# The first tap of 44 blocks moves from VectorE to ScalarE, and VectorE sums the second rows of all pairs 1 to 47

## The chip, the cores and the metric

One NeuronCore of a Trainium2 chip runs the whole program. The metric is the device time of one launch in microseconds: before the change the median of three runs is 2565.99 us (2560.9 to 2567.07). TensorE multiplies matrices into PSUM, VectorE (DVE) and ScalarE (ACT) work elementwise, GpSimd (POOL) issues the gathers of rows, SyncE (SP) issues the loads of weights. The engines run side by side and meet at semaphores.

## What the reference computes

Two transformer blocks over 512 positions of width 1024. The part that matters here is the gated feed-forward of the first block,

```
up = causal_dwconv(h2 @ ffn_w_up, ffn_conv_w, ffn_conv_b)   # 3 taps, 5632 columns
a, b = split(up);  x = x + gate2 * ((silu(a) * b) @ ffn_w_down)
```

and the expert layer at the end of the second, in which every position and each of 8 heads picks 16 of 16384 experts:

```
u = expert_u[experts];  act = gelu(sum_d u * h);  v = expert_v[experts]
out = sum_k gate_k * act_k * v_k
```

## The kernel before

The sequence is worked on in two halves of 256 positions. The first half runs ahead: its expert layer begins while the second half still has its first block's feed-forward to do. That work of the second half is put between the steps of the expert layer, by tables written out by hand.

The unit of the expert layer is a **pair** p: two gathered rows per position (each a 128x2048 f32 tile, `expert_u` and `expert_v` side by side, 1.05 MB), 16 choices of a head make 8 pairs, 256 pairs in all. GpSimd gathers rows 2p and 2p+1 into a ring of 9 slots (`ring_e`); it may refill a slot when its old row has been used. VectorE forms the row products of both rows (`row_dot`, L2267). ScalarE turns them into weights and into diagonal matrices (`weigh_pair`, L1467 to L1478). TensorE adds diagonal times row into two PSUM banks (`row_pair`): two products of 128x512 for each row, each of them two records of the trace. For a pair that stands in the table `SIDE` TensorE does the first row only, ScalarE makes one diagonal only, and VectorE adds weight times second row to an SBUF tile, two pairs later (`side_row`, 128x1024); TensorE takes that tile in once for every 64 pairs. Before the change `SIDE` holds 1 to 23, then every other pair from 25 to 39, then 40 to 47, and some later ones.

After its part of pair p every engine does what the tables put **beside** it. `UP_AT` places the 44 up blocks of the second half: three blocks in two pairs, in pairs 1 to 16 and 22 to 35 (odd pairs two, even pairs one, with small exceptions). `DOWN_AT` places 24 down blocks in pairs 17 to 21 and 35 to 45. For an up block m at pair `UP_AT[m]`:

- TensorE multiplies it (`expand`, 128x258, 16 records), into one of three PSUM banks in turn. It waits for the weights, which SyncE loads when the block three before is done (`half_done`, three slots `w2`), and for the bank, until the block three before has been read out (`evicted`: for an up block `fy_ready`).
- VectorE at `UP_AT[m]` + 2 applies the three taps of the convolution from PSUM (`expanded`): one `tensor_scalar` with the bias, then two `scalar_tensor_tensor`; the last counts `fy_ready`.
- ScalarE at + 3 takes the tanh for the gate (`tanh_gate`), VectorE at about + 4 multiplies gate and value (`gate_value`).

Each engine works in this order strictly. So VectorE, which waits in `expanded` for the end of a block of TensorE two pairs back, can be two pairs ahead of TensorE and no more. From pair 48 on there are further such blocks, and later stages only have the expert layer.

Of the kernel before, what the change touches and what calls it, by code (L numbers as in the profile page):

```python
# [15 lines left out]
ACT = mybir.ActivationFunctionType  # L16
# [15 lines left out]
FT = FF // P  # L32
# [13 lines left out]
HF = S // 2  # L46
# [37 lines left out]
def ffn_at(i):  # L84

    return 1 + 2 * i // 3


UP_AT = [ffn_at(b if b < 24 else b + KT) for b in range(2 * FT)]
# [10 lines left out]
            {m: 102 + 2 * m if m < 4 else 112 + 4 * (m - 4) for m in range(16)}]  # L100


SIDE = [*range(1, 24), *range(25, 40, 2), *range(40, 48), *range(56, 62), *range(83, 88, 2), *range(88, 96)]


def sides(p):

    return sum(q < p for q in SIDE)


def by_tensor(g):

    return g - sum(2 * q + 1 < g for q in SIDE)

# [25 lines left out]
TURN = {b: t for t, b in enumerate(ORDER)}  # L140
# [32 lines left out]
def build(nc, a, out):  # L173
    ctx = ExitStack()
    with ctx:
# [33 lines left out]
        def par(name, i=0, n=1):  # L209
            b = PARAM[name][0] + i  # L210
            return param[:, b:b + n]
# [78 lines left out]
        yg = wring[:, 3072:3584].rearrange("p (u n) -> p u n", n=HF)  # L290
        yv = wring[:, 3584:4096].rearrange("p (u n) -> p u n", n=HF)
# [44 lines left out]
        PS = ctx.enter_context(nc.psum_tensor("PS", [P, 8, S], F32))  # L336
# [7 lines left out]
        half_done = sem("half_done")  # L344
# [23 lines left out]
        ff_ready = sem("ff_ready")  # L368
# [67 lines left out]
        qkv_ready = sem("qkv_ready")  # L436
# [26 lines left out]
        vec_step = sem("vec_step")  # L463
# [32 lines left out]
        def bank(name, half, m):  # L496
            return 2 + TURN[name, half, m] % SLOTS2
# [54 lines left out]
        def _(pe):  # L552
# [446 lines left out]
            def row_pair(p, start, stop):  # L999
# [3 lines left out]
                if start:  # L1003
                    pe.wait_ge(hr_ready, 4)
                    if p:
                        pe.wait_ge(prow_ready, 2 * (p // TILE))
                rows = range(1 if p in SIDE else BATCH)
                for k in rows:
# [128 lines left out]
        def _(act):  # L1137
            n = Count()
            A = nc.scalar.activation
# [217 lines left out]
            def square_block(s, k):  # L1357
# [6 lines left out]
                    act.wait_ge(sq3_used, SUMS3[s] + k - 3)  # L1364
                A(sq4[:, k % 4, :], xT[:, k, HF:] if s else xT[:, k, :HF], ACT.Square).then_inc(sq3_ready, 1)

            def tanh_gate(t):

                act.wait_ge(fy_ready, 2 * FT + 2 * t + 1)
                if t >= 2:  # L1370
                    act.wait_ge(ff_ready, FT + t - 1)
                A(st[t % 2], yg[:, t % 2, :], ACT.Tanh, scale=0.5).then_inc(sa_ready, 1)
# [6 lines left out]
            def apply3(s):  # L1379

                shift, col = (0, 2) if s == 1 else (24, 3)
                if s == 0:
                    act.wait_ge(mod_ready, 4)
                for k in range(KT):
                    act.wait_ge(normed3, KT * s + k + 1)
                    h = hv[:, 1, k, :] if s else hv[:, 0, k, :]
                    A(h, h, ACT.Identity, bias=mod[:, 1, shift + k:shift + k + 1], scale=eff[:, col, k:k + 1]).then_inc(h3_ready, 1)
# [73 lines left out]
            def weigh_pair(p, r):  # L1461

                b = p % NB
                act.wait_ge(dots_ready, BATCH * (p + 1))
                if p - NB in SIDE:
                    act.wait_ge(side_used, sides(p - NB + 1))
# [5 lines left out]
                act.wait_ge(w_ready2, BATCH * p + 1)  # L1472
                if p in SIDE:
                    A(diag[:, b, 0, :], ident, ACT.Copy, scale=wts[:, b, 0:1]).then_inc(diag_ready, 1)
# [32 lines left out]
            def beside(p):  # L1507

                c, q = divmod(p, TILE)
                if c and q == 0:  # L1510
                    keep_tile(c - 1)
                if p == 3:
                    keep_scores(0, EARLY - 1)
                for s in range(2):
                    for m, at in QUERY_AT[s].items():
                        if p == at + 2:
                            keep_query(s, m)
                        if p == at + 5:
                            keep_scores(s, m)
                for m, at in enumerate(WIN_AT):  # L1520
                    if p == at + 2:
                        keep_block(1, m)
                for g, at in enumerate(POOL_AT):
                    if p == at + 2:
                        keep_pool(1, g)
                if p == LN_AT + 2:
                    keep_mean(1)
                if p == LN_AT + 3:
                    ln_squares(1)
                if p == LN_AT + 6:  # L1530
                    ln_root(1)
                if p == LN_AT + 7:
                    ln_tanh(1)
                for m, at in enumerate(WOUT_AT):
                    if p == at + 2:
                        square_block(2, m)
                if p == NORM_AT + 2:
                    root3(2)
                if p == NORM_AT + 3:
                    apply3(2)  # L1540
                for t in range(FT):
                    if p == UP_AT[2 * t] + 3:
                        tanh_gate(t)
                for m, at in enumerate(DOWN_AT):
                    if m // KT == CHUNKS - 1 and p == at + 2:
                        square_block(1, m % KT)
                if p == MID_AT + 2:
                    root3(1)
                if p == MID_AT + 3:
                    apply3(1)  # L1550
                if p - 2 in BROW_AT:
                    keep_brow(BROW_AT.index(p - 2))
                if p - 2 in XROW_AT:
                    keep_x(*XROW_AT[p - 2])
                if p - 2 in FIN_AT:
                    deviation(FIN_AT[p - 2])
                if 0 < c < NC - 1 and q == 50:
                    keep_rows(c + 1, 0, 7)
                if 0 < c < NC - 1 and q == 53:
                    keep_rows(c + 1, 1, 7)  # L1560
# [21 lines left out]
        def _(dve):  # L1582
            n = Count()
# [5 lines left out]
            def ts(o, x, s1, s2, op0, op1):  # L1589
                return V.tensor_scalar(o, x, s1, s2, op0, op1)  # L1590
# [21 lines left out]
            MUL, ADD, SUB, MAX, MIN = ALU.mult, ALU.add, ALU.subtract, ALU.max, ALU.min  # L1612
# [358 lines left out]
            for i in range(FT // 2):  # L1971
                ada_steps(4 * i, 4 * i + 4)
                for u in range(2):
                    for z in range(2):
# [3 lines left out]
                        o = (y0 if z == 0 else y1)[:, u, :]  # L1978
# [141 lines left out]
            def expanded(m):  # L2120

                t, z = divmod(m, 2)
                o, b = (yg, yv)[z][:, t % 2, :], bank("up", 1, m)
                dve.wait_ge(half_done, TURN["up", 1, m] + 1)
                ts(o, PS[:, b, 2:HF + 2], par("fconv", 3 * m + 2), par("fbias", m), MUL, ADD).then_inc(vec_step, 1)
                dve.wait_ge(vec_step, n(vec_step))
                stt(o, PS[:, b, 1:HF + 1], par("fconv", 3 * m + 1), o, MUL, ADD).then_inc(vec_step, 1)
                dve.wait_ge(vec_step, n(vec_step))
                stt(o, PS[:, b, 0:HF], par("fconv", 3 * m), o, MUL, ADD).then_inc(fy_ready, 1)
                dve.wait_ge(fy_ready, n(fy_ready))  # L2130
# [196 lines left out]
            def beside(p):  # L2327

                c, q = divmod(p, TILE)
                if p - 2 in SIDE:  # L2330
                    side_row(p - 2)
                for g in range(4):
                    if p == WIN_AT[g] + 3:
                        pool_diff(1, g)
                for t in range(4):
                    if p == WIN_AT[5 + 2 * t] + 3:
                        gated(1, t)
                for i, at in enumerate(DW_AT):
                    if p == at:
                        tap(1, i)  # L2340
                if p == LN_AT + 3:
                    ln_center(1)
                if p == LN_AT + 7:
                    ln_scale(1)
                if p == LN_AT + 8:
                    ln_silu(1)
                for m, at in enumerate(BRANCH_AT):
                    if p == at + 2:
                        merge(1, m)
                for m, at in enumerate(WOUT_AT):  # L2350
                    if p == at + 2:
                        add_block(1, m)
                if p == NORM_AT + 3:
                    norm3(2)
                if p == MID_AT + 3:
                    norm3(1)
                for t in range(FT):
                    if p == max(UP_AT[2 * t] + 4, UP_AT[2 * t + 1] + 3):
                        gate_value(t)
                for m, at in enumerate(UP_AT):  # L2360
                    if p == at + 2:
                        expanded(m)
                for m, at in enumerate(DOWN_AT):
                    if p == at + 2:
                        add_part(m)
                if p in FIN_AT:
                    finish(FIN_AT[p])
                if p - 3 in FIN_AT:
                    scale_rows(FIN_AT[p - 3])
# [183 lines left out]
```

## Time and profile before

| | |
|---|---|
| median of three runs | 2565.99 us |
| profiled execution | 2566.99 us, span 2565.3 us |
| TensorE busy | 2293.6 us (89%) |
| VectorE busy | 1719.5 us (67%) |
| ScalarE busy | 695.7 us (27%) |
| GpSimd busy | 618.9 us (24%) |
| moved by DMA | 748.97 MB, mean 292 GB/s |
| chain that ended last | PE 62%, DMA 23%, DVE 9%, ACT 4% |

The span is the time from the first to the last instruction. "Busy" is the time in which an engine executes. The chain is followed back from the last instruction, at each step to what released it, so its shares say what the time was spent on. In the 40 equal slices of the page (64 us each) the expert layer begins in the seventeenth, at 1023 us; pair 24 begins on TensorE at 1243 us, pair 40 at 1368 us, pair 48 at 1412 us.

### The profile page before, as it was taken

The numbers are of one execution on the slowest core, as the hardware profiler recorded it, in microseconds if no ns is written. First come the engines' busy times: TensorE is split into PE (matmuls) and PEld (weight loads), VectorE is DVE, ScalarE is ACT, GpSimd is POOL, SyncE is SP. The second block draws the span as 40 slices with busy tenths as digits, with TensorE's granted clock in tenths as the row PEclk, the third lists the DMA queues.
The fourth block names the chain that finished last, engine by engine and source line by source line (L and its number), as shares of the span: only waits on it lengthen the run. The fifth ranks groups of instructions, "written<-read, shape, count | busy, mean of one in ns | idle before, by whom it ended". The sixth has DMA issues, their size and how long they took to land.

```text
span 2565.3 us, 25633 instructions
## 1 busy us (share of the span) xinstructions
PE 2293.6 (89%) x8418; PEld 1491.4 (58%) x8418; DVE 1719.5 (67%) x3782; ACT 695.7 (27%) x1990; POOL 618.9 (24%) x612
## 2 busy tenths in 40 slices
PE   3999998899999998899999998999998877777776
PEld 2544685748888887677777565675444433232222
DVE  6753564617655853778887799877667666676664
ACT  2221122413101111221222322424333333333332
POOL 2100000000001000222332333434444434344342
PEclk7999997899999999999999999999999999999999
DMA  8621102025666433999999999999999999999997
GB/s 304 228 80 57 33 1 66 1 98 197 237 219 240 148 128 124 388 343 369 409 374 390 392 380 371 376 410 409 419 419 419 420 420 420 418 418 420 419 418 295
DMA packets 130584, 748.97 MB, mean 292 GB/s; under 512 B 14497, under 2 KB 14497, under 8 KB 64673
## 3 DMA queue, kind: packets, MB, share of 16 engines
q0 software_dynamic: 87552, 587.24, 57.4%
q1 hardware_dynamic: 42912, 160.26, 17.6%
q8 instruction: 60, 0.98, 0.2%
q14 instruction: 60, 0.48, 0.1%
HBM read 745.35 MB, written 2.10 MB: 291 GB/s over the span
## 4 chain that ended last, share of the span: by engine, by line
PE 62%; DMA 23%; DVE 9%; ACT 4%; issue 2%; another core or an unknown queue 0%; POOL 0%; DVEq 0%; ACTq 0%; POOLq 0%
PE PS L554 61%; DMA arena<-experts_dram,ecur 21%; DVE arena L2267 3%; DVE h_all L1593 2%; DMA arena<-ada_dram 1%; DVE arena L1593 1%; ACT arena L1471 1%; DVE arena L1587 1%; ACT L1467 1%; DVE h_all L1587 1%; ACT const L1478 0%; ACT const L1476 0%; DMA ring<-up_dram 0%; DMA ring<-down_dram 0%; ACT arena L1467 0%
## 5 line engine op out<-in xcount | busy, mean ns | idle before, releaser
L554 PE MATMUL PS<-arena,const 128*128 128x512 f32 (+2 forms) x1872 | 879.5, 614 | 179.6 <-ACT const L1478 165.6
L554 PE MATMUL PS<-h_all,ring 128*128 128x256 f32 (+2 forms) x3584 | 884.2, 405 | 10.5 <-ACT h_all L1166 4.0
L2426 POOL DMA_INDIRECT arena<-experts_dram,ecur x512 | 567.8, 1109 | 1162.7 <-PE PS L554 758.8
L2267 DVE CUSTOM_DVE_ANT_0 arena<-arena 128x1024 f32<-128x1024 f32 x512 | 626.0, 1223 | 293.5 <-DMA arena<-experts_dram,ecur 289.3
L554 PEld LDWEIGHTS PS<-h_all,ring 128*128 128x128 f32 x3584 | 681.8, 191 | 221.7 <-issue 135.6
L554 PEld LDWEIGHTS PS<-arena,const 128*128 128x128 f32 (+1 forms) x1872 | 353.6, 195 | 626.2 <-issue 361.4
L1467 ACT ACTIVATE arena<-arena 128x2 f32<-128x2 f32 x255 | 51.8, 203 | 846.9 <-DVE arena L2267 846.5
L554 PE MATMUL PS<-arena,ring 128*128 128x256 f32 (+1 forms) x960 | 245.3, 417 | 3.7 <-DVE arena L1587 2.6
L554 PEld LDWEIGHTS PS<-arena,ring 128*128 128x128 f32 x960 | 186.8, 195 | 63.9 <-issue 36.6
L554 PE MATMUL PS<-arena 128*128 128x128 f32 (+2 forms) x1088 | 157.1, 305 | 8.6 <-DVE arena L1587 3.5
L554 PEld LDWEIGHTS PS<-arena 128*128 128x128 f32 (+1 forms) x1088 | 143.4, 208 | 28.2 <-issue 8.4
L1593 DVE SCALAR_TENSOR_TENSOR arena<-arena,silc 128x512 f32<-128x512 f32 x168 | 126.3, 752 | 18.0 <-DMA arena<-ada_dram 12.3
L1471 ACT ACTIVATE arena<-arena 128x1 f32<-128x1 f32 x510 | 122.3, 287 | 8.4
L1593 DVE SCALAR_TENSOR_TENSOR xT<-PS,mod,xT 128x256 f32<-128x256 f32 (+1 forms) x56 | 29.0, 520 | 128.3 <-PE PS L554 128.2
L2408 POOL DMA_DIRECT2D arena<-ada_dram x4 | 2.1, 528 | 384.6 <-ACT arena L1294 384.6
L1587 DVE TENSOR_TENSOR arena<-arena 128x256 f32<-128x256 f32 (+9 forms) x185 | 86.4, 467 | 5.4 <-ACT arena L1212 2.7
L2413 POOL DMA_DIRECT2D arena<-ada_dram x44 | 23.2, 528 | 266.3 <-DVE arena L1593 266.3
L1478 ACT ACTIVATE const<-const,arena 128x128 f32<-128x128 f32 x199 | 76.8, 386 | 0.0
L1476 ACT ACTIVATE const<-const,arena 128x128 f32<-128x128 f32 x199 | 76.8, 386 | 0.0
L1593 DVE SCALAR_TENSOR_TENSOR arena<-arena 128x1024 f32<-128x1024 f32 (+3 forms) x93 | 75.8, 815 | 0.6 <-ACT arena L1471 0.3
L1590 DVE TENSOR_SCALAR arena<-PS,param 128x256 f32<-128x256 f32 (+1 forms) x56 | 32.9, 588 | 58.8 <-PE PS L554 57.8
L1593 DVE SCALAR_TENSOR_TENSOR arena<-PS,param,arena 128x255 f32<-128x255 f32 (+3 forms) x124 | 69.4, 559 | 4.4
(246 smaller groups left out, 1591.0 us busy)
## 6 DMA issues: line engine op xcount, KB each, us to landing
arena<-ada_dram POOLq DMA_DIRECT2D x96, 512.0 KB, 5.2
ring<-up_dram SPq DMA_DIRECT2D x88, 512.0 KB, 3.5
ring<-w_in_dram SPq DMA_DIRECT2D x80, 512.0 KB, 3.6
ring<-query_dram SPq DMA_DIRECT2D x32, 512.0 KB
ring<-w_out_dram SPq DMA_DIRECT2D x24, 512.0 KB, 4.0
ring<-down_dram SPq DMA_DIRECT2D x16, 704.0 KB, 4.9
ring<-branch_dram SPq DMA_DIRECT2D x16, 512.0 KB
arena<-experts_dram,ecur POOLq DMA_INDIRECT x512
```

The lines of the kernel that those rows point to most:

```text
L554: return nc.tensor.matmul(o, l, r, start=start, stop=stop)
L1467: A(wts[:, b, :], dots[:, b, :], ACT.Gelu_apprx_tanh).then_inc(gelu_ready, 1)
L1471: A(wts[:, b, k:k + 1], wts[:, b, k:k + 1], ACT.Copy, scale=gcur[:, r % 3, j:j + 1]).then_inc(w_ready2, 1)
L1476: A(diag[:, b, 0, :], ident, ACT.Copy, scale=wts[:, b, 0:1]).then_inc(act_step, 1)
L1478: A(diag[:, b, 1, :], ident, ACT.Copy, scale=wts[:, b, 1:2]).then_inc(diag_ready, 1)
L1587: return V.tensor_tensor(out=o, in0=x, in1=y, op=op)
L1590: return V.tensor_scalar(o, x, s1, s2, op0, op1)
L1593: return V.scalar_tensor_tensor(out=o, in0=x, scalar=s_, in1=y, op0=op0, op1=op1)
L2267: V.tensor_tensor_reduce(out=u, in0=u, in1=hrow[:, (r // HEADS) % 2, :], scale=1.0, scalar=0.0, op0=MUL, op1=ADD, accum_out=dots[:, p % NB ...
L2408: pool.dma_start(ring_2[:, j, :], a["ada_2"][j]).then_inc(slot_2_ready[j], 16)
L2413: pool.dma_start(ring_2[:, j, :], a["ada_2"][bass.ds(i * SLOTS + j, 1)].rearrange("o p n -> p (o n)")).then_inc(slot_2_ready[j], 16)
L2426: nc.gpsimd.indirect_dma_start(out=ring_e[:, g % RING, :], out_offset=None, in_=a["experts"], in_offset=bass.IndirectOffsetOnAxis(ap=ecur[ ...
```

## The change

The table `SIDE` now holds all pairs 1 to 47, so the eight even pairs 24 to 38 are added: TensorE leaves their second rows out, VectorE sums them. The first tap with the bias is done by ScalarE with an `Identity` activation from PSUM (`up_tap`), at `UP_AT[m]` + 2. VectorE does the other two taps at + 3, after a wait for ScalarE's tap instead of TensorE's block. `gate_value` stands at + 4 after the later of the two blocks.

```diff
-SIDE = [*range(1, 24), *range(25, 40, 2), *range(40, 48), *range(56, 62), *range(83, 88, 2), *range(88, 96)]
+SIDE = [*range(1, 48), *range(56, 62), *range(83, 88, 2), *range(88, 96)]
@@ ScalarE
+            def up_tap(m):
+
+                t, z = divmod(m, 2)
+                act.wait_ge(half_done, TURN["up", 1, m] + 1)
+                if t >= 2:
+                    act.wait_ge(ff_ready, FT + t - 1)
+                A((yg, yv)[z][:, t % 2, :], PS[:, bank("up", 1, m), 2:HF + 2], ACT.Identity, bias=par("fbias", m),
+                  scale=par("fconv", 3 * m + 2)).then_inc(qkv_ready, 1)
...
+                for m, at in enumerate(UP_AT):
+                    if p == at + 2:
+                        up_tap(m)
@@ VectorE
-                dve.wait_ge(half_done, TURN["up", 1, m] + 1)
-                ts(o, PS[:, b, 2:HF + 2], par("fconv", 3 * m + 2), par("fbias", m), MUL, ADD).then_inc(vec_step, 1)
-                dve.wait_ge(vec_step, n(vec_step))
+                dve.wait_ge(qkv_ready, 12 + m + 1)
                 stt(o, PS[:, b, 1:HF + 1], par("fconv", 3 * m + 1), o, MUL, ADD).then_inc(vec_step, 1)
...
-                    if p == max(UP_AT[2 * t] + 4, UP_AT[2 * t + 1] + 3):
+                    if p == max(UP_AT[2 * t], UP_AT[2 * t + 1]) + 4:
                         gate_value(t)
                 for m, at in enumerate(UP_AT):
-                    if p == at + 2:
+                    if p == at + 3:
                         expanded(m)
```

TensorE's queue at pairs 23 to 26, before (`PS<-arena,const` are the rows times diagonals, x2 for one row and x4 for two; `PS<-h_all,ring` are up blocks, 8 products each):

```order
L554 MATMUL PS<-h_all,ring 128x258 x16
L554 MATMUL PS<-arena,const 128x512 x4
L554 MATMUL PS<-h_all,ring 128x258 x8
L554 MATMUL PS<-arena,const 128x512 x2
L554 MATMUL PS<-h_all,ring 128x258 x16
L554 MATMUL PS<-arena,const 128x512 x4
```

and after:

```order
L554 MATMUL PS<-h_all,ring 128x258 x16
L554 MATMUL PS<-arena,const 128x512 x2
L554 MATMUL PS<-h_all,ring 128x258 x8
L554 MATMUL PS<-arena,const 128x512 x2
L554 MATMUL PS<-h_all,ring 128x258 x16
L554 MATMUL PS<-arena,const 128x512 x2
```

Each even pair has lost two products of 128x512; the blocks stand where they stood.

VectorE's queue at pair 26, from its second row product on, before (`arena<-arena 128x1024` by ISA is the row product, `ring<-arena,ring` and `arena<-ring` the gate times value, `ring<-PS,param` the first tap, `ring<-PS,param,ring` the others):

```order
L2267 ISA arena<-arena 128x1024
L2267 ISA arena 128x1
L1596 CAST arena<-icur 128x32
L1587 TENSOR_TENSOR arena<-arena 128x256
L1593 SCALAR_TENSOR_TENSOR ring<-arena,ring 128x256
L1587 TENSOR_TENSOR arena<-ring 128x256
L1590 TENSOR_SCALAR ring<-PS,param 128x256
L1593 SCALAR_TENSOR_TENSOR ring<-PS,param,ring 128x256 x2
```

and after:

```order
L2277 ISA arena<-arena 128x1024
L2277 ISA arena 128x1
L1608 CAST arena<-icur 128x32
L1599 TENSOR_TENSOR arena<-arena 128x256
L1605 SCALAR_TENSOR_TENSOR arena<-arena 128x1024
L1605 SCALAR_TENSOR_TENSOR ring<-PS,param,ring 128x256 x4
```

The sum of pair 24's second row has come in, the gate times value now follows later, the first tap is gone, and the taps that stand here are those of the two blocks of pair 23 instead of the block of pair 24.

ScalarE's queue at pairs 24 and 25, before (`arena<-arena 128x2` is the gelu, `const<-const,arena` a diagonal, `arena<-ring` the tanh):

```order
L1467 ACTIVATE arena<-arena 128x2
L1471 ACTIVATE arena<-arena 128x1 x2
L1476 ACTIVATE const<-const,arena 128x128
L1478 ACTIVATE const<-const,arena 128x128
L1467 ACTIVATE arena<-arena 128x2
L1471 ACTIVATE arena<-arena 128x1 x2
L1474 ACTIVATE const<-const,arena 128x128
L1372 ACTIVATE arena<-ring 128x256
```

and after:

```order
L1476 ACTIVATE arena<-arena 128x2
L1480 ACTIVATE arena<-arena 128x1 x2
L1483 ACTIVATE const<-const,arena 128x128
L1373 ACTIVATE ring<-PS,param 128x256
L1476 ACTIVATE arena<-arena 128x2
L1480 ACTIVATE arena<-arena 128x1 x2
L1483 ACTIVATE const<-const,arena 128x128
L1373 ACTIVATE ring<-PS,param 128x256 x2
L1381 ACTIVATE arena<-ring 128x256
```

The second diagonal of pair 24 is gone, and the taps of the blocks two pairs back stand between one pair's diagonal and the next pair's gelu.

## Rows read from the trace of the kernel before

**Rows 1.** Chain of waits, 1030 to 1420 us: start, length (us), what.

```profile
1058.35 9.47 DMA ring<-up_dram
...
1103.76 276.60 PE PS L554 x1116
...
1380.38 9.30 DMA ring<-down_dram
...
1389.72 15.37 PE PS L554 x62
...
1412.63 11.47 DMA arena<-experts_dram,ecur
```

**Rows 2.** Stretches: length, busy us of each engine, PEclk, DMA share, GB/s.

```profile
1165.00:1243.00 78.00, 78.00 (x322) 60.30 (x321) 71.75 (x157) 19.42 (x63) 22.33 (x23) 1.00 1.00 398
1214.00:1268.00 54.00, 54.00 (x211) 39.74 (x210) 43.99 (x98) 11.51 (x38) 18.06 (x15) 1.00 1.02 418
1243.00:1368.00 125.00, 125.00 (x483) 91.37 (x482) 99.97 (x226) 26.18 (x88) 41.40 (x32) 1.00 0.99 382
1268.00:1382.00 114.00, 114.00 (x445) 84.09 (x444) 91.66 (x206) 24.84 (x82) 36.29 (x30) 1.00 0.98 373
1382.00:1455.00 73.00, 64.99 (x201) 38.86 (x200) 60.08 (x142) 30.84 (x86) 27.82 (x26) 0.93 1.01 417
1900.00:2100.00 200.00, 171.48 (x477) 87.75 (x475) 133.82 (x337) 71.01 (x234) 82.78 (x76) 0.98 1.01 419
```

**Rows 3.** Timeline of TensorE, pairs 28 to 31: start, us, what.

```profile
1278.10 3.65 PE L554 MATMUL PS<-h_all,ring 128*128 128x258 f32 x16
1281.59 1.88 PE L554 MATMUL PS<-arena,const 128*128 128x512 f32 x4
1283.31 7.14 PE L554 MATMUL PS<-h_all,ring 128*128 128x258 f32 x32
1290.29 3.59 PE L554 MATMUL PS<-arena,const 128*128 128x512 f32 x8
1293.72 3.65 PE L554 MATMUL PS<-h_all,ring 128*128 128x258 f32 x16
```

**Rows 4.** Timeline of VectorE, 1276 to 1298 us.

```profile
1276.56 1.22 DVE L2267 CUSTOM_DVE_ANT_0 arena<-arena 128x1024 f32<-128x1024 f32 x1
...
1281.87 0.54 DVE L1590 TENSOR_SCALAR ring<-PS,param 128x256 f32<-128x256 f32 x1 [0.71 <-PE PS L554]
1282.44 1.00 DVE L1593 SCALAR_TENSOR_TENSOR ring<-PS,param,ring 128x256 f32<-128x256 f32 x2
1283.48 1.23 DVE L2267 CUSTOM_DVE_ANT_0 arena<-arena 128x1024 f32<-128x1024 f32 x1
...
1286.66 1.28 DVE L1593 SCALAR_TENSOR_TENSOR arena<-arena 128x1024 f32<-128x1024 f32 x1
1287.86 0.42 DVE L1593 SCALAR_TENSOR_TENSOR ring<-arena,ring 128x256 f32<-128x256 f32 x1
```

**Rows 5.** ScalarE: activations from PSUM with a bias; a pair's weights.

```profile
L1328 ACT ACTIVATE arena<-PS,param x32: 452/474/475, 876.1 to 1644.1; 128x256 f32<-128x256 f32 x32
1279.79 0.20 ACT L1467 ACTIVATE arena<-arena 128x2 f32<-128x2 f32 x1 [7.87 <-DVE arena L2267]
```

**Rows 6.** Timeline of TensorE, pairs 15 and 16.

```profile
1179.43 1.88 PE L554 MATMUL PS<-arena,const 128*128 128x512 f32 x4
1181.15 7.14 PE L554 MATMUL PS<-h_all,ring 128*128 128x258 f32 x32
1188.13 1.88 PE L554 MATMUL PS<-arena,const 128*128 128x512 f32 x4
1189.84 3.65 PE L554 MATMUL PS<-h_all,ring 128*128 128x258 f32 x16
1193.33 1.88 PE L554 MATMUL PS<-arena,const 128*128 128x512 f32 x4
```

**Rows 7.** Timeline of VectorE, first row products of pairs 16, 17 and 18.

```profile
1177.29 1.22 DVE L2267 CUSTOM_DVE_ANT_0 arena<-arena 128x1024 f32<-128x1024 f32 x1
...
1183.31 1.24 DVE L2267 CUSTOM_DVE_ANT_0 arena<-arena 128x1024 f32<-128x1024 f32 x1
...
1192.21 1.23 DVE L2267 CUSTOM_DVE_ANT_0 arena<-arena 128x1024 f32<-128x1024 f32 x1
```

**Rows 8.** Waits, 1268 to 1382 us: us in total, times, longest.

```profile
POOL arena L2426 <- PE PS L554: 49.3, 16, 4.2
POOL arena L2426 <- DVE arena L1593: 24.3, 9, 3.1
```

## The prediction

> **What bounds the kernel now.** I read the chain of waits first, since it says what the time of each stretch was spent on. From 1103.76 us on it is 276.60 us of TensorE in one piece [rows 1]; that covers pairs 6 to 42, the stretch in which the changed pairs 24 to 39 lie. Ahead of it stands a load of up weights, behind it a load of down weights, 15.37 us more of TensorE, and then the landing of a gather. So TensorE is the bound where the change acts, and DMA soon after it.
>
> Then the stretches [rows 2]. TensorE is busy all of 1165 to 1382 us at full clock, which agrees. But look at the last two columns. The DMA share reads 0.98 to 1.02 everywhere, so it can't tell a full DMA side from one that has a little room; the rate can. It is 417 to 419 GB/s in 1214:1268, in 1382:1455 and in 1900:2100, where TensorE is idle 14% of the time, and 373 in 1268:1382. I read 418 as what the engines can move of this mix of gathers and weights, and 373 as what TensorE asks for. The waits support it: in 1268:1382 GpSimd waits 49.3 us for TensorE and 24.3 us for VectorE to free a slot [rows 8]; the demand is short there, not the supply.
>
> **TensorE.** A pair with one row holds 4 records of 128x512, from 1281.59 to 1283.31, 1.72 us; one with two rows has 8, from 1290.29 to 1293.72, 3.43 us [rows 3]. The difference is 1.71 us. Eight pairs (24, 26, ... 38) lose it: 8 x 1.71 = 13.7 us, all on the chain. This is the most that the change can remove.
>
> **What is late next.** In 1268:1382 there are 373 GB/s x 114 us = 42.5 MB to move. At 418 GB/s this takes 101.7 us, so the DMA side can follow by 12.3 us and not by 13.7. Another way to see it: pairs 24 to 39 (1243:1368) move 382 x 125 = 47.8 MB; in 125 - 13.7 = 111.3 us that would be 429 GB/s, above every rate in the rows. Nor will every microsecond of the 12.3 be found, since the DMA side can only be full if slots always come free in time. The nearest row for that is 1165:1243, where all pairs already have one row on TensorE and VectorE has the side sums: 398 GB/s. At 398 the 42.5 MB take 106.8 us, a gain of 7.2. The two ends are 7.2 and 12.3. I take the middle, 9.7: 398 includes a beginning in which TensorE had no need of more (it was busy 78 of 78 us), and against 418 stands that with equal paces of two sides some time is always lost. After 1382 the rate is 417 up to 1455, so a shift of the DMA side is kept as it is, and one of TensorE alone is lost: TensorE is idle 8.0 of the 73 us of 1382:1455 as it is [rows 2].
>
> By the Trainium skill (DMA: Bandwidth & Descriptors, section "Where 436 GB/s comes from") the HBM side limits a core at about 358 GB/s. By that the stretch at 373 would be over the limit already and the change would bring nothing. This case's trace disagrees, with 419 GB/s held over 200 us [rows 2]; I go by the row.
>
> **VectorE.** The first tap costs 1281.87 to 1282.44 = 0.57 us from start to start; 44 of them go, 25.1 us. A side sum costs 1286.66 to 1287.86 = 1.20 us; eight come, 9.6 us [rows 4]. Net 15.5 us less, off the chain, so worth nothing by itself. It decides whether VectorE can keep the new pace. With side sums in every pair VectorE needed 1177.29 to 1192.21 = 14.9 us for two pairs with three blocks, with no wait in between [rows 7], and TensorE 1179.43 to 1193.33 = 13.9 [rows 6]; VectorE was the slower there. Without three taps it is 14.9 - 3 x 0.57 = 13.2. The DMA side has 4 rows of 1.05 MB and 3 blocks of 0.52 MB, 5.77 MB, at 418 GB/s 13.8 us. So 13.2, 13.8 and 13.9 us for two pairs: the side sums of all pairs fit, with 5% to spare, which is why the two parts of the change belong together.
>
> **ScalarE.** 44 taps; the nearest row is an activation from PSUM with a bias, 0.47 us [rows 5], 20.7 us in all, less eight diagonals. ScalarE is busy 26.18 us of 125 in pairs 24 to 39 [rows 2], and idle 7.87 us before the gelu at 1279.79 [rows 5]. The tap waits for a block of TensorE two pairs back, and behind it are queued the tanh and the gelu and diagonal of the next pair. TensorE needs that diagonal only after the blocks of one more pair and its rows, over 5 us later by [rows 6] (1188.13 to 1193.33), and the taps and a pair's weights take about 2. I count 0. If the cover went, two taps of 0.47 would show in every second pair, about 1 us each for 24 pairs.
>
> **Moved steps.** The bank of an up block is released one pair later. TensorE takes it for the block three on, two pairs after, so at its pair p it now needs VectorE through with what stands beside p + 1, that is about to begin the row products of p + 2. Before: at pair 28 the block starts at 1278.10 and VectorE began pair 30 at 1276.56, 1.5 us ahead; at pair 29 it is 1283.31 against 1283.48 [rows 3, 4], where the first of the two blocks is through about 1 us before the end, so 0.9 ahead. VectorE waited for TensorE there (0.71 us before the tap), and that wait is now ScalarE's, one pair sooner in VectorE's order. So it will be further ahead, and I count 0 for the stalls. GpSimd's and SyncE's order does not change; slots of the second rows of the eight pairs are freed by VectorE at p + 2 instead of TensorE at p, about when VectorE starts beside TensorE's next pair. Nothing taken, bounds 0 and 1.2 us a pair, within the 7.2.
>
> **Sum.** -9.7 on the profiled execution's 2566.99 us gives 2557.3; that execution is 1.0 us over the median of the runs, so by the median 2565.99 - 9.7 = 2556.3. About 0.3% (7.7 us) is what a measurement of this kernel can tell from no change.
>
> **The rivals.**
> 1. *TensorE alone counts.* The DMA side is ahead enough, because 1214:1268 already ran at 418 and filled the slots, and a VectorE that is less late frees slots sooner. Then all 13.7 us are won: 2552.3. Against it: the 429 GB/s.
> 2. *The DMA side is full already,* as its share of 0.98 says, or the room is used up by pair 40 and TensorE's lead given back in pairs 40 to 47. Gain 0 to 7 us, centre 2562. Against it: 418 next to 373 at the same share; for it: the even paces above, and TensorE's 8.0 us idle behind it.
> 3. *The bank becomes the wait, and it is slower.* In pairs 13 to 17 VectorE was late: the block of pair 15 starts at 1181.15 and VectorE begins pair 17 at 1183.31, 2.2 us later; at pair 16 1189.84 against 1192.21, 2.4 [rows 6, 7]. Under the old order that cost nothing, under the new one TensorE stands for it. If VectorE is as late as that in all pairs whose block needs a bank of an up block and that have no other blocks to wait with (13 to 17 and 24 to 37, 19 pairs), it is 19 x 2.2 = 42 us less 13.7: 2594. It breaks even at 0.7 us a pair. Against it: VectorE's 13.2 against 13.9 us.
>
> **Chances.** The forecast, a gain that the DMA side limits to 7.2 to 12.3 us: 0.50 (its own range 2553.7 to 2558.8). Rival 1: 0.14. Rival 2: 0.28. Rival 3: 0.08. Faster by over 0.3%, that is under 2558.3: rival 1 and nearly all of the forecast, 0.14 + 0.44 = 0.58. Within 0.3%: 0.06 + 0.28 = 0.34. Slower: 0.08. The range goes from below rival 1's 2552.3, by the scatter of the runs, to no gain: 2551 to 2566.
>
> **What would show it.** In the profile after: TensorE 13.7 us less busy (32 records of 128x512 less); pairs 24 to 39 about 10 to 12 us shorter; the rate there near 415 GB/s instead of 382; VectorE still without waits for landings in most pairs, and no longer waiting for TensorE in the taps; ScalarE with 44 more activations of 0.47 us that wait for TensorE and delay nothing. Wrong would be: a chain in pairs 13 to 39 that passes through VectorE's last tap (rival 3), a rate under 400 with gaps in TensorE (rival 2), or pair 48 reached 13 us or more sooner (rival 1).

## The result, and the profile after

The changed kernel runs in 2549.43 us (median of 6 runs, 2544.73 to 2553.06) against 2565.09 for the one before (6 runs). The ratio is 0.9945 with a 95% interval of 0.9932 to 0.9958, or 14.1 us less (10.8 to 17.4); the two medians are 15.7 us apart. The forecast was 9.7 us less, with 7.2 to 12.3 as the likeliest case's own range, and 2551 as the lower end of all: the direction is right, the forecast gain is too small, and the measured median lies below the whole range. The profiled execution took 2552.48 us, 14.5 less than that of before.

The page after, busy time by engine: TensorE 2281.9 instead of 2293.6, VectorE 1706.2 instead of 1719.5, ScalarE 717.1 instead of 695.7. TensorE has the 32 records less that were forecast (8386 instead of 8418), and 11.7 us less busy time instead of 13.7; the stretch of pairs 24 to 39 shows the 13.7.

```profile
PE 2281.9 (89%) x8386; PEld 1485.2 (58%) x8386; DVE 1706.2 (67%) x3746; ACT 717.1 (28%) x2026; POOL 621.5 (24%) x612
```

The stretches after answer to [rows 2], with the same columns. The first two have the same place as before, the others are moved by what was won up to there; the third and the fourth answer to 1243:1368 and 1268:1382.

```profile
1165.00:1243.00 78.00, 78.00 (x324) 60.53 (x323) 63.69 (x146) 22.24 (x66) 26.64 (x22) 1.00 1.01 407
1214.00:1268.00 54.00, 54.00 (x219) 41.22 (x218) 47.43 (x102) 15.74 (x47) 18.21 (x16) 1.00 1.02 418
1243.00:1354.00 111.00, 111.00 (x450) 84.90 (x449) 97.96 (x210) 34.03 (x100) 34.54 (x32) 1.00 1.02 417
1268.00:1368.00 100.00, 100.00 (x404) 76.16 (x403) 86.62 (x190) 28.87 (x86) 28.98 (x28) 1.00 1.02 415
1368.00:1441.00 73.00, 63.19 (x198) 38.21 (x197) 58.97 (x138) 30.41 (x84) 26.15 (x25) 0.95 1.01 415
```

Pairs 24 to 39 take 111.0 us, TensorE is busy for all 111, and the rate is 417 GB/s. That is 13.7 us less than 124.7: the whole of TensorE's part. The two lengths come from TensorE's timelines, from the start of pair 24 to the start of pair 40. Before:

```profile
1243.44 3.60 PE L554 MATMUL PS<-arena,const 128*128 128x512 f32 x8
1368.12 1.88 PE L554 MATMUL PS<-arena,const 128*128 128x512 f32 x4
```

And after:

```profile
1242.96 1.88 PE L554 MATMUL PS<-arena,const 128*128 128x512 f32 x4
1353.97 1.88 PE L554 MATMUL PS<-arena,const 128*128 128x512 f32 x4
```

So the DMA side did follow. One more column matters: in 1165:1243, where TensorE does the same as before, the rate is 407 instead of 398 and VectorE's busy time 63.69 instead of 71.75. The waits of GpSimd for VectorE's sums to free a slot (us in total, times, longest) fell there. Before:

```profile
POOL arena L2426 <- DVE arena L1593: 45.7, 12, 5.8
```

After:

```profile
POOL arena L2436 <- DVE arena L1605: 14.4, 6, 3.0
```

The chain of waits, 1030 to 1420 us, against [rows 1]: TensorE in one piece from 1094.46 to 1379 us, and behind it landings of gathers; the load of down weights that stood there before is no longer in it.

```profile
1094.46 284.92 PE PS L554 x1168
...
1379.64 14.22 DMA arena<-experts_dram,ecur
...
1398.35 13.17 DMA arena<-experts_dram,ecur
```

TensorE's timeline at pairs 28 to 30, against [rows 3]: every pair has four records of 128x512 now, and a pair with one block takes 1284.66 to 1289.86 = 5.2 us. An even pair with one block had taken 3.43 + 3.49 = 6.9 us.

```profile
1277.68 7.14 PE L554 MATMUL PS<-h_all,ring 128*128 128x258 f32 x32
1284.66 1.88 PE L554 MATMUL PS<-arena,const 128*128 128x512 f32 x4
1286.37 3.65 PE L554 MATMUL PS<-h_all,ring 128*128 128x258 f32 x16
1289.86 1.88 PE L554 MATMUL PS<-arena,const 128*128 128x512 f32 x4
```

VectorE's timeline there, against [rows 4]: there is no first tap, the four later taps of two blocks stand in one row, VectorE has no wait, and the row product at 1274.42 is the first of pair 31.

```profile
1271.15 1.28 DVE L1605 SCALAR_TENSOR_TENSOR arena<-arena 128x1024 f32<-128x1024 f32 x1
1272.34 2.04 DVE L1605 SCALAR_TENSOR_TENSOR ring<-PS,param,ring 128x256 f32<-128x256 f32 x4
1274.42 1.22 DVE L2277 CUSTOM_DVE_ANT_0 arena<-arena 128x1024 f32<-128x1024 f32 x1
```

The first block of pair 29 starts at 1277.68, so VectorE is 3.3 us ahead of what the bank needs, where it was about 0.9 by the old order. At pair 15, where VectorE would have been 2.2 us too late by the new order [rows 6, 7], it is ahead now. VectorE's timeline, the first product of pair 17:

```profile
1175.21 1.22 DVE L2277 CUSTOM_DVE_ANT_0 arena<-arena 128x1024 f32<-128x1024 f32 x1
```

TensorE's timeline there, the two blocks beside pair 15:

```profile
1180.67 7.14 PE L554 MATMUL PS<-h_all,ring 128*128 128x258 f32 x32
```

VectorE starts pair 17 at 1175.21 and the block starts at 1180.67: the bank is free 5.5 us before it is needed.

ScalarE's taps by their source line (least, median and largest ns of one, then first and last start): the median is 564 ns instead of the 474 that I took, 44 x 564 ns = 24.8 us in all.

```profile
L1373 ACT ACTIVATE ring<-PS,param x44: 546/564/567, 1057.4 to 1323.1; 128x256 f32<-128x256 f32 x44
```

One of them in ScalarE's timeline, with the idle time ahead of it and what ended it in brackets: the wait for TensorE's block is ScalarE's now.

```profile
1284.86 0.57 ACT L1373 ACTIVATE ring<-PS,param 128x256 f32<-128x256 f32 x1 [2.92 <-PE PS L554]
```

### The profile page after: what moved, and what is told of

Same layout as the page of the kernel before. It is cut to its first block, busy times and chain, and to the rows that moved or that the text cites. A ratio compares the mean times of both kernels' runs of the same rounds, so it can differ in the third digit from the quotient of the medians.

```text
span 2550.8 us, 25625 instructions
## 1 busy us (share of the span) xinstructions
PE 2281.9 (89%) x8386; PEld 1485.2 (58%) x8386; DVE 1706.2 (67%) x3746; ACT 717.1 (28%) x2026; POOL 621.5 (24%) x612
## 4 chain that ended last, share of the span: by engine, by line
PE 61%; DMA 24%; DVE 9%; ACT 4%; issue 2%; another core or an unknown queue 0%; POOL 0%; DVEq 0%; ACTq 0%; POOLq 0%
PE PS L554 60%; DMA arena<-experts_dram,ecur 21%; DVE arena L2277 3%; DVE h_all L1605 2%; DVE arena L1605 1%; DMA arena<-ada_dram 1%; DVE arena L1599 1%; ACT L1476 1%; ACT arena L1480 1%; DVE h_all L1599 0%; ACT const L1487 0%; ACT const L1485 0%; DMA ring<-up_dram 0%; DMA ring<-query_dram 0%; DMA ring<-w_out_dram 0%
## 5 line engine op out<-in xcount | busy, mean ns | idle before, releaser
L554 PE MATMUL PS<-arena,const 128*128 128x512 f32 (+2 forms) x1840 | 868.5, 616 | 176.6 <-ACT const L1487 163.0
L1605 DVE SCALAR_TENSOR_TENSOR arena<-arena,silc 128x512 f32<-128x512 f32 x168 | 126.3, 752 | 17.0 <-DMA arena<-ada_dram 11.5
L1605 DVE SCALAR_TENSOR_TENSOR xT<-PS,mod,xT 128x256 f32<-128x256 f32 (+1 forms) x56 | 29.1, 521 | 126.8 <-PE PS L554 126.5
L1605 DVE SCALAR_TENSOR_TENSOR arena<-arena 128x1024 f32<-128x1024 f32 (+3 forms) x101 | 86.1, 852 | 0.3
L1487 ACT ACTIVATE const<-const,arena 128x128 f32<-128x128 f32 x191 | 73.7, 386 | 0.0
L1485 ACT ACTIVATE const<-const,arena 128x128 f32<-128x128 f32 x191 | 73.6, 386 | 0.0
```

The costliest lines, as they stand in the source:

```text
L554: return nc.tensor.matmul(o, l, r, start=start, stop=stop)
L1487: A(diag[:, b, 1, :], ident, ACT.Copy, scale=wts[:, b, 1:2]).then_inc(diag_ready, 1)
L1605: return V.scalar_tensor_tensor(out=o, in0=x, scalar=s_, in1=y, op0=op0, op1=op1)
```

## The experiments

Each ratio is to executions of the kernel before on the same chip and beside that kernel, so the ratios can be compared; medians of kernels that ran on different chips can't. The times by stage come from TensorE's timelines of one profiled execution each, from the first 128x512 record of a pair to that of another. "Idle at 48" is how long TensorE stood idle ahead of pair 48; in the kernel before and in the changed one it is the first idle time of over 1 us behind the changed pairs. The rate is that between the starts of pairs 13 and 24. The two executions of the changed kernel are 0.8 us apart in pairs 40 to 47 and 2.2 us in pairs 48 to 52, so less than that says nothing.

| kernel | ratio to before (95%) | GB/s, 13 to 24 | pairs 24 to 39 | pairs 40 to 47 | idle at 48 | pairs 48 to 61 |
|---|---|---|---|---|---|---|
| before | 1 | 396 | 124.7 | 43.9 | 2.2 | 98.3 |
| changed | 0.9945 (0.9932 to 0.9958) | 406 | 111.0 | 43.9 | 3.0 | 98.9 |
| changed, again | 0.9955 (0.9941 to 0.9970) | 406 | 111.0 | 43.1 | 2.2 | 98.0 |
| side sums only | 0.9964 (0.9951 to 0.9977) | 396 | 110.9 | 47.9 | 6.3 | 99.2 |
| taps only | 0.9992 (0.9982 to 1.0002) | 408 | 124.7 | 43.1 | 2.2 | 96.8 |
| taps not moved | 0.9941 (0.9926 to 0.9956) | 402 | 110.9 | 43.9 | 2.9 | 101.0 |
| taps early | 0.9959 (0.9947 to 0.9971) | 405 | 110.9 | 48.6 | 6.6 | 96.0 |
| taps late | 0.9957 (0.9943 to 0.9970) | 396 | 111.0 | 44.7 | 3.7 | 101.6 |
| lean TensorE | 0.9946 (0.9931 to 0.9961) | 406 | 108.9 | 46.2 | 4.0 | 100.2 |
| lean on both | 0.9925 (0.9911 to 0.9939) | 398 | 104.8 | 43.4 | 2.2 | 99.2 |
| more side sums | 0.9926 (0.9911 to 0.9941) | 407 | 111.0 | 43.1 | 2.2 | 95.0 |
| all to 61 | 0.9956 (0.9941 to 0.9971) | 407 | 111.0 | 42.8 | 2.1 | 94.9 |

### Side sums only

```diff
 # the kernel before, with
+SIDE = [*range(1, 48), *range(56, 62), *range(83, 88, 2), *range(88, 96)]
```

> The kernel before with the eight pairs added to SIDE and nothing else: all three taps stay on VectorE, two pairs behind the block. Theory A (the two parts need each other): VectorE, which took 14.9 us for two pairs with side sums and three blocks where TensorE took 13.9, becomes the bound in pairs 24 to 39; they take about 8 x 14.4 = 115 to 119 us instead of 124.7, so 6 to 9 us are won and 5 to 8 of the 13.7 are missing. Rival B (VectorE's lead of some 13 us carries it through 16 pairs, each of which loses only 0.5 us): pairs 24 to 39 take 111 us and the time is 12 to 14 us under before, the same as with the whole change.

Measured: 0.9964, about 9.2 us less (5.9 to 12.6). Neither theory holds as written: pairs 24 to 39 take 110.9 us, so VectorE does not become the bound there, as the rival said, but 4.0 us are given back in pairs 40 to 47. The stretches and the waits say why. In pairs 24 to 39 VectorE is busy 107.76 of 111 us, GpSimd waits 67.3 us for VectorE's sums to free slots, and the rate is 407 instead of 417. The first line is pairs 13 to 23, the second pairs 24 to 39.

```profile
1163.30:1242.10 78.80, 78.80 (x325) 60.87 (x325) 72.17 (x157) 19.47 (x63) 22.39 (x23) 1.00 0.99 396
1242.10:1353.10 111.00, 111.00 (x450) 85.02 (x450) 107.76 (x233) 23.91 (x81) 32.28 (x31) 1.00 1.01 407
```

```profile
POOL arena L2426 <- DVE arena L1593: 67.3, 15, 6.4
```

The debt shows at pair 48, in TensorE's timeline: it waits 6.29 us for the diagonal of a row product that came late.

```profile
1400.94 2.07 PE L554 MATMUL PS<-arena,const 128*128 128x512 f32 x2 [6.29 <-ACT const L1478]
```

The chain of waits names what was late. VectorE's side sum ends at 1379.06 and frees a slot, GpSimd fills it, and the landing, 15.94 us long, is what that row product had to wait for.

```profile
1377.83 1.20 DVE arena L1593
...
1379.78 0.94 POOL arena L2426
...
1381.03 15.94 DMA arena<-experts_dram,ecur
```

In the changed kernel TensorE frees the slot there, not VectorE, and the same wait is 2.96 us.

```profile
1397.83 2.07 PE L554 MATMUL PS<-arena,const 128*128 128x512 f32 x2 [2.96 <-ACT const L1487]
```

### Taps only

```diff
 # the changed kernel, with
+SIDE = [*range(1, 24), *range(25, 40, 2), *range(40, 48), *range(56, 62), *range(83, 88, 2), *range(88, 96)]
```

> The whole change but with the old SIDE: the first tap on ScalarE and the other taps a pair later, no second row moved. Both theories: TensorE stays the bound in pairs 24 to 39 (124.7 us) and nothing is won, 0 +- 2 us to before. What it tells is whether VectorE's earlier position (in the changed kernel it leads by 17 to 29 us in pairs 4 to 18 instead of 10 to 20) moves bytes ahead: if it does, the rate in 1165:1243 is near 407 GB/s as in the changed kernel, if that came from the side sums of the later pairs it is 398 as before.

Measured: 0.9992, no difference, and pairs 24 to 39 take 124.7 us as before. The rate between pairs 13 and 24 is 408 GB/s as in the changed kernel.

```profile
1163.10:1241.90 78.80, 78.80 (x325) 60.84 (x324) 64.38 (x146) 23.17 (x68) 26.72 (x23) 1.00 1.01 408
```

So the taps bring nothing by themselves, and it is they that move bytes ahead: (408 - 396) GB/s x 78.8 us = 0.95 MB. GpSimd's wait for VectorE's sums is 14.5 us there, as in the changed kernel, instead of 45.7. And the 398 GB/s on which I built the low end was no limit of the DMA side.

```profile
POOL arena L2436 <- DVE arena L1605: 14.5, 6, 3.0
```

### Taps not moved

```diff
 # the changed kernel, with
-                    if p == at + 3:
+                    if p == at + 2:
                         expanded(m)
```

(and `gate_value` where it was before).

> The whole change without the move by one pair: ScalarE's tap and VectorE's other two taps both two pairs behind the block. Theory A (only the side sums and the relief of VectorE count): VectorE again waits for the end of a block two pairs back, now through ScalarE, its lead is held at 12 to 13 us, but TensorE is still the bound: within 1.5 us of the changed kernel, 12 to 14 us under before. Rival B (the lead that the later taps allow moved bytes ahead and so let DMA follow by 13.7 instead of 12.3 us): 1 to 3 us are missing, and pair 40 is reached that much later than in the changed kernel.

Measured: 0.9941. Pairs 24 to 39 take 110.9 us, and TensorE is idle 2.9 us at pair 48, the same as with the move. That is theory A. The move by one pair is worth nothing here. It is the relief of VectorE that counts, not its further lead.

### More side sums

```diff
 # the changed kernel, with
-SIDE = [*range(1, 48), *range(56, 62), ...]
+SIDE = [*range(1, 48), *range(53, 62), ...]
```

> The changed kernel with pairs 53, 54 and 55 also in SIDE, where TensorE is busy from 1427 on and leads are over 20 us. Theory A (one second row off TensorE is worth 1.71 us wherever TensorE is the chain): 3 x 1.71 = 5.1 us under the changed kernel, about 18.8 under before. Rival B (what is won there is lost in pairs 62 to 72, where TensorE waits for weights again and DMA sets the pace at 380 to 410 GB/s): under 2 us.

Measured: 0.9926, 19.0 us under before (15.1 to 22.8). From pair 53 to pair 62 it takes 65.5 us, the changed kernel 69.8 (71.1 in the second run); from pair 24 to the last pair 1291.6 us, the changed kernel 1297.0 and 1296.0. That is theory A, by the trace; the interval of the whole time still overlaps that of the changed kernel (0.9932 to 0.9958). The changed kernel between the starts of pairs 53 and 62:

```profile
1426.90:1496.70 69.80, 69.80 (x277) 52.34 (x276) 55.94 (x130) 18.97 (x58) 20.20 (x18) 1.00 0.96 369
```

The same pairs with more side sums:

```profile
1427.70:1493.20 65.50, 65.18 (x266) 49.95 (x265) 58.11 (x131) 17.98 (x55) 19.34 (x19) 1.00 0.99 387
```

In the changed kernel TensorE was busy all the time there and the rate was 369, well under 417: where both hold, a row off TensorE counted in full.

### All to 61

```diff
 # the changed kernel, with
+SIDE = [*range(1, 62), *range(83, 88, 2), *range(88, 96)]
```

> The changed kernel with all of pairs 48 to 55 in SIDE as well. Pairs 53 to 55 are worth 5.1 us, as the run with them alone showed. Theory A (in pairs 48 to 52 the chain goes through landings and VectorE, TensorE is idle): the other five bring nothing or cost up to their side sums on VectorE, 5 x 1.2 = 6 us: pairs 48 to 53 take 29 to 35 us instead of 29.1. Rival B (a row off TensorE always brings 1.7 us): 8.5 us more, pairs 48 to 53 in 21 us.

Measured: 0.9956. Pairs 48 to 52 take 29.4 us, as in the changed kernel (29.1) and with the side sums of pairs 53 to 61 alone (29.5), though TensorE has five second rows less. That is theory A: where TensorE waits, a row off it brings nothing. TensorE is busy 16.10 us of it:

```profile
1395.40:1424.90 29.50, 16.10 (x25) 5.62 (x25) 26.16 (x58) 11.96 (x31) 12.50 (x10) 0.71 0.92 368
```

With those five rows still on TensorE (more side sums, 1398.2 to 1427.7 us) it is busy 23.55 us of the same length.

The ratio of the whole is above that of more side sums (0.9926), but the two ran on different chips and their medians are 0.6 us apart (2547.24 and 2546.65); in the trace this kernel takes 2.0 us more from pair 24 to the last.

### Lean TensorE, and lean on both sides

```diff
 # the changed kernel, with
-                for k in range(KT):
+                n_ = KT - 1 if m >= 24 else KT
+                for k in range(n_):
                     ins = mm(PS[:, bank("up", 1, m), :HF + 2], w[k], hf[:, k, :], ...)
 # and, for both sides,
+                elif name == "up" and m >= 24:
+                    sp.dma_start(w2[:, t % SLOTS2, 0:5 * P], a[name][m][:, 0:5 * P])...
```

> The changed kernel with one of eight products left out in each of the 20 up blocks 24 to 43 (pairs 22 to 35; so part of those blocks' sums is missing). TensorE has 20 x 0.43 = 8.6 us less there. Theory A (after the change the DMA side is full at 417 GB/s, so the next microsecond off TensorE brings nothing): the time is within 2 us of the changed kernel, and TensorE shows gaps or a shrinking lead in pairs 24 to 47. Rival B (418 GB/s was no limit, as the prediction's cap of 12.3 us was none): 7 to 9 us less than the changed kernel.

> The same with the weight loads of these 20 blocks cut to five of eight columns as well (the rest of the slot holds old numbers), 3.9 MB or 9.4 us of DMA at 418 GB/s less. Theory A: now both sides have room, and most of the 8.6 us is won, 6 to 9 us under the changed kernel. Rival B: the same as the run with the lean TensorE alone, within 1.5 us.

> The changed kernel once more, on the same chip as the two lean ones, to compare with them: 13 to 15 us under before in the stretches of the trace, 12 to 16 in the time.

These two kernels leave work out, so their results are not the layer's. The lean TensorE does seven of the eight products in each of the 20 up blocks 24 to 43; lean on both sides also loads only five eighths of their weights.

Measured: the lean TensorE alone has 0.9946 next to 0.9955, no gain clear of the intervals. Lean on both sides has 0.9925, and from pair 13 to pair 48 it takes 225.7 us against 232.9 of the changed kernel run beside it, 7.2 of the 8.6 us. With TensorE alone it is 232.6. So the changed kernel stands right at the edge: TensorE's work and the DMA's take about equal times, and the next microsecond must come off both. Lean weights with TensorE as it is, the fourth corner, was not run. The stretch of pairs 24 to 39 with the lean TensorE:

```profile
1239.00:1347.90 108.90, 105.02 (x415) 77.94 (x414) 99.60 (x213) 34.69 (x100) 34.21 (x32) 1.00 1.02 417
```

The same with both lean, where TensorE idles less:

```profile
1233.60:1338.40 104.80, 104.03 (x415) 78.27 (x414) 98.73 (x213) 34.81 (x100) 33.34 (x32) 1.00 1.02 413
```

With the lean TensorE the waits of that stretch show the wait of the prediction's third rival, in small: VectorE waits 4.1 us for landings, and TensorE waits 3.4 us for VectorE's last taps to release banks. That the one makes the other is my reading of them.

```profile
DVE arena L2278 <- DMA arena<-experts_dram,ecur: 4.1, 7, 0.9
PE PS L554 <- DVE ring L1606: 3.4, 3, 1.8
```

The changed kernel, run again, took 0.9955, 11.5 us less (7.7 to 15.1). This is a little under the 12 to 16 expected and overlaps the first result; from pair 24 to pair 48 it takes 14.5 us less than the kernel before, as expected.

### Taps early, taps late

ScalarE's tap only for blocks 0 to 23, or only for blocks 24 to 43; the others as before. Of the edit only VectorE's part is shown; ScalarE skips the taps that aren't its own, and the other taps and the gate stand where they stood before.

```diff
 # the changed kernel, with
+TAPPED = [m for m in range(2 * FT) if m < 24]     # late: m >= 24
+                if m in TAPPED:
+                    dve.wait_ge(qkv_ready, 12 + TAPPED.index(m) + 1)
+                else:
+                    dve.wait_ge(half_done, TURN["up", 1, m] + 1)
+                    ts(o, PS[:, b, 2:HF + 2], par("fconv", 3 * m + 2), par("fbias", m), MUL, ADD).then_inc(vec_step, 1)
```

> All side sums of the change, but ScalarE's first tap only for up blocks 0 to 23 (pairs 1 to 16); blocks 24 to 43 as before. Theory A (two shares: the relief before pair 24 moves 0.8 MB or 1.9 us ahead, the relief in pairs 24 to 39 keeps VectorE fast enough to free slots, worth 1.07 MB or 2.6 us): 407 GB/s in 1165:1243, pairs 24 to 40 in 111.0 us, but 1 MB behind, and 2 to 3 us are missing in pairs 40 to 48; pair 24 to 53 takes 185.5 to 187 us. Rival B (all of the 4.0 us that the side sums alone gave back in pairs 40 to 48 came from VectorE's pace in 24 to 39): 187.5 or more, as the side sums alone (186.7).

> The complement: ScalarE's tap only for blocks 24 to 43. Theory A: 398 GB/s in 1165:1243, pairs 24 to 40 in 111.0 us, 1 to 2 us missing against the changed kernel by pair 53 (24 to 53 in 185 to 186 us), since the DMA side starts 0.8 MB behind. Rival B: nothing missing, 24 to 53 in 184 us.

Measured: 0.9959 and 0.9957. The intervals overlap with one another and with those of the side sums alone and of the whole change, so the verdict is the trace's. From pair 24 to pair 48 the changed kernel takes 154.9 and 154.1 us, taps late 155.7, taps early 159.5, side sums only 158.8. Taps early, in pairs 24 to 39:

```profile
1238.50:1349.40 110.90, 110.90 (x449) 84.97 (x448) 107.72 (x233) 23.90 (x81) 32.23 (x31) 1.00 1.00 401
```

Taps late, in the pairs before them:

```profile
1160.80:1239.60 78.80, 78.80 (x326) 60.87 (x325) 71.90 (x160) 20.14 (x64) 23.16 (x23) 1.00 0.99 396
```

The same kernel in pairs 24 to 39:

```profile
1239.60:1350.60 111.00, 111.00 (x449) 84.91 (x448) 99.31 (x212) 34.70 (x100) 37.48 (x32) 1.00 1.02 417
```

So what the side sums alone give back at pair 48, 4 to 5 us, is VectorE's pace in pairs 24 to 39, where it is busy 107.72 of 110.9 us: taps early, with that pace and the bytes ahead, gives back as much. The bytes moved ahead before pair 24 are worth 0.8 to 1.6 us at most, by taps late. The two executions of the changed kernel differ by 0.8 us themselves, and taps early, which has these bytes, is 0.7 us behind the side sums alone, so their worth is not shown. I had expected 2.6 and 1.9.

By pair 53 the early taps have 73.4 us from pair 40, the late 74.9, the changed kernel 73.0 and 70.0. There my expectation for the early taps (24 to 53 in 185.5 to 187 us) failed, and so did its rival (187.5 or more): it is 184.3, because pairs 48 to 52 took 24.8 us. The late taps have 185.9, as expected. What decides pairs 48 to 52 is open: at a mean granted clock of 0.87 to 0.88 they take 24.8 us with the early taps, 26.9 with the taps alone and 29.1 in the changed kernel.

## Why the prediction was wrong

**What bounds the kernel: right.** TensorE was the chain, its 13.7 us went, and the measured stretch shows them one for one: 124.7 to 111.0. Pair 48 was reached 13.7 us sooner counted from pair 24, which the prediction had named as the sign of the first rival.

**"What is late next": this step failed.** It let the DMA side follow by 7.2 to 12.3 us and put 9.7 into the sum; the runs show 13.7 to 14.5 at pair 48. Three things in it were off.
- The low end of 7.2 us came from reading 398 GB/s in 1165:1243 as what the DMA side gives when all pairs have side sums. It was what was asked of it: VectorE, at 14.9 us for two pairs, freed slots late, and GpSimd waited 45.7 us for it. With the taps alone moved, this wait is 14.5 us and the stretch runs at 408.
- So the middle, 9.7, priced a VectorE as loaded as before, which I had myself worked out to be gone (13.2 us for two pairs). The run with that VectorE, side sums only, has 9.2 us, and 9.8 to pair 48 in the trace (168.6 - 158.8). Its rate was 407 GB/s, by which the prediction's 42.5 MB take 104.4 us, a gain of 9.6. The forecast was in effect that for half of the change. I had called VectorE's relief worth nothing by itself, which is right (0.9992), and then left it out of the sum for the whole, which is wrong: next to the side sums it is worth 4 to 5 us at pair 48. In the whole time the intervals of the two kernels overlap, so this rests on the traces.
- The upper end took the 42.5 MB as fixed to the stretch. Pairs 24 to 39 moved 382 x 124.7 = 47.6 MB before and 417 x 111.0 = 46.3 MB after, and TensorE never stood for the missing 1.3 MB. Some had moved ahead: the relief before pair 24 is worth 0.7 to 0.9 MB, some 2 us at 418 GB/s. But taps late, without these bytes, also takes 111.0 us for 46.3 MB, so the stretch does not need them. The rest is moved behind it: pairs 40 to 47 ran at 403 GB/s before and at 413 after. Without the bytes ahead 12.9 us arrive at pair 48, with them 13.7 and 14.5.

Pairs 40 to 47 before:

```profile
1368.10:1412.00 43.90, 41.09 (x157) 29.29 (x155) 37.23 (x81) 13.33 (x41) 13.76 (x14) 1.00 1.01 403
```

And after:

```profile
1354.00:1397.80 43.80, 40.87 (x157) 29.34 (x155) 36.11 (x75) 13.34 (x41) 13.05 (x14) 1.00 1.01 413
```

About 418 as the limit of the DMA side agrees with the runs. None of the changed kernel's stretches above is faster, and with TensorE lean the time stays where it is unless bytes go too.

**"With equal paces some time is always lost": not seen.** TensorE is busy 111.00 of 111.00 us at 417 GB/s. The nine slots were enough of a buffer, as I read it; no run had fewer or more.

**The rivals.** The first, to which I gave 0.14, is what happened, and by the reason named there: a VectorE that is less late frees slots sooner. The second did not come as priced: TensorE's idle time in the stretch behind is 9.8 of 73 us instead of 8.0, and at pair 48 it is 3.0 us instead of 2.2 in the first profile and 2.2 in the second, so at most a microsecond or two of the lead was given back. The third did not come either: TensorE has no wait in pairs 24 to 39, and VectorE was 3.3 and 5.5 us ahead of the two banks looked at. The wait itself exists, as the lean TensorE shows.

**The smaller terms.** VectorE: 13.3 us less on the page, 15.5 forecast from starts. ScalarE hides its taps as said, at 564 ns instead of 474. The move by one pair costs nothing and, as the run without it shows, brings nothing. The gain was kept behind pair 48: from the start of pair 24 to that of pair 53 the kernel before takes 197.1 us and the changed one 183.9, and to the last pair 1311.0 and 1297.0.

## What to carry to other kernels

A rate below the best seen is a demand until another engine's column says otherwise; before it is used as a limit, look at who frees the buffers in that stretch, and whether the change touches that engine. When a change has two parts, one of which is worth nothing alone, work out the sum with both in place: the relief of an engine off the chain can be what lets the other part arrive. And moving work off the bound engine paid in full here in the stretches in which it was busy all the time and the transfers were under their best rate, and nothing where it waited.

## What the runs showed that I had not expected

The same kernel's executions differ by up to 10 us before the expert layer begins. The changed kernel's first row product starts at 1037.5 us in one profile and at 1027.3 in the other; some 6 of these 10 us arise between 390 and 465 us, where the granted clock differs. The changed kernel's first profile there:

```profile
400.00:500.00 100.00, 87.12 (x461) 65.62 (x460) 57.31 (x173) 36.22 (x144) 0.00 (x0) 0.82 0.13 43
```

The same stretch in its second profile:

```profile
400.00:500.00 100.00, 85.12 (x494) 66.48 (x493) 61.77 (x186) 38.61 (x153) 0.00 (x0) 0.89 0.14 43
```

The clock is 0.82 in the first and 0.89 in the second. The kernel is the same there, so this is scatter, and larger than most differences here; it is why the experiments are read by stage. In pairs 40 to 52, too, the same kernel took 73.0 us at a mean clock of 0.95 and 70.0 at 0.98, with TensorE idle for 9.8 and 8.5 us of it. What decides the clock there was not tried.
